# Norm factors with one token per partition, and spread back by a matmul with the identity

## The reference

```python
def rms_norm(x, g):
    xf = x.astype(jnp.float32)
    y = xf * lax.rsqrt(jnp.mean(xf * xf, axis=-1, keepdims=True) + NORM_EPS)
    return (y * g.astype(jnp.float32)).astype(x.dtype)
```

## Time and profile before

| | |
|---|---|
| median of 3 runs | 3188.65 us (3179.95 to 3190.11) |
| the profiled execution | 3185.06 us, span of its instructions 3183.4 us |
| mean granted clock | 0.978 |
| TensorE busy | 3001.6 us, 94% of the span |
| VectorE busy | 2112.0 us, 66% |
| ScalarE busy | 1008.0 us, 32% |
| chain that ended last | PE 88%, DVE 6%, ACT 3% |

### The profile page before, as it was taken

How to read it: one execution, slowest core, us unless ns; L and a number is a source line. 1 busy time by engine, 2 the same in 40 slices (tenths; PEclk the granted TensorE clock), 3 DMA queues, 4 the chain that set the end, 5 groups by cost and what they waited for, 6 DMA issues and landing times.

```text
span 3183.4 us, 46595 instructions
## 1 busy us (share of the span) xinstructions
PE 3001.6 (94%) x18188; PEld 2552.6 (80%) x18188; DVE 2112.0 (66%) x3065; ACT 1008.0 (32%) x1091; POOL 95.1 (3%) x154
## 2 busy tenths in 40 slices
PE   6999988999999999998999999989899989998898
PEld 4888856888868887784899899858779979985898
DVE  7877778667686766546566766646556666664466
ACT  5222223222232222314434444311033334342333
POOL 0000020000000000000000000000000000000000
PEclk9999999999999999999999999989999989999999
DMA  8444322434433433320345344400034554442244
GB/s 337 158 164 165 132 86 99 152 119 162 154 119 119 157 140 123 127 85 1 115 185 185 132 174 173 147 0 1 1 100 170 197 139 158 185 158 33 94 170 171
DMA packets 68214, 421.03 MB, mean 132 GB/s; under 512 B 7576, under 2 KB 8728, under 8 KB 25856
## 3 DMA queue, kind: packets, MB, share of 16 engines
q1 hardware_dynamic: 48416, 344.41, 29.3%
q0 software_dynamic: 19712, 75.41, 7.3%
HBM read 418.71 MB, written 1.07 MB: 132 GB/s over the span
## 4 chain that ended last, share of the span: by engine, by line
PE 88%; DVE 6%; ACT 3%; issue 1%; DMA 1%; SPq 0%; ACTq 0%; DVEq 0%
PE ps_o L1582 11%; PE ps_o L1584 10%; PE ps_o L1583 10%; PE ps_g L1582 7%; PE ps_u L1582 7%; PE ps_u L1584 7%; PE ps_g L1584 7%; PE ps_u L1583 7%; PE ps_g L1583 7%; PE ps_o L1589 2%; PE ps_g L1597 2%; PE ps_o L1775 1%; PE ps_o L1997 1%; DVE wlo L919 1%; ACT whi L605 1%
## 5 line engine op out<-in xcount | busy, mean ns | idle before, releaser
L605 ACT ACTIVATE whi<-wraw 128x2048 fp32r<-128x2048 f32 x326 | 622.2, 1912 | 1035.4 <-PE ps_u L1584 419.3
L919 DVE TENSOR_TENSOR wlo<-wraw,whi 128x2048 fp32r<-128x2048 f32 x326 | 738.6, 2289 | 211.0 <-ACT whi L605 210.7
L1582 PE MATMUL ps_o<-ah,wlo 128*128 128x256 f32 (+1 forms) x1408 | 468.9, 333 | 17.0 <-issue 15.4
L1582 PE MATMUL ps_g<-hh,wlo 128*128 128x256 f32 (+1 forms) x1408 | 460.0, 327 | 21.2 <-DVE hl L963 13.8
L1582 PE MATMUL ps_u<-hh,wlo 128*128 128x256 f32 (+1 forms) x1408 | 458.9, 326 | 0.0
L1584 PE MATMUL ps_o<-ah,whi 128*128 128x256 f32 (+1 forms) x1408 | 458.4, 326 | 0.0
L1584 PE MATMUL ps_u<-hh,whi 128*128 128x256 f32 (+1 forms) x1408 | 457.7, 325 | 0.0
L1583 PE MATMUL ps_o<-al,whi 128*128 128x256 f32 (+1 forms) x1408 | 457.7, 325 | 0.0
L1584 PE MATMUL ps_g<-hh,whi 128*128 128x256 f32 (+1 forms) x1408 | 457.2, 325 | 0.0
L1583 PE MATMUL ps_u<-hl,whi 128*128 128x256 f32 (+1 forms) x1408 | 456.8, 324 | 0.0
L1583 PE MATMUL ps_g<-hl,whi 128*128 128x256 f32 (+1 forms) x1408 | 456.4, 324 | 0.0
(11 more groups left out here) (381 smaller groups left out, 3890.5 us busy)
## 6 DMA issues: line engine op xcount, KB each, us to landing
wraw<-in_W SPq DMA_DIRECT2D x327, 1024.0 KB, 4.8
scr<-in_ADA POOLq DMA_DIRECT2D x120, 512.0 KB, 3.7
scr<-bias_rows POOLq DMA_DIRECT2D x8, 384.0 KB, 7.9
x<-in_XT POOLq DMA_DIRECT2D x1, 2048.0 KB, 10.6
x<-in_MEMT POOLq DMA_DIRECT2D x2, 1024.0 KB, 7.6
cst<-in_CST POOLq DMA_DIRECT2D x1, 1799.5 KB, 7.2
cst<-in_CB POOLq DMA_DIRECT2D x1, 1024.0 KB, 7.0
out<-x SPq DMA_DIRECT2D x1, 1024.0 KB, 4.8
```

Of the source, the lines that this page charges most:

```text
L605: nc.scalar.activation(whi[:, n % SLOTS, :], wraw[:, n % SLOTS, :], ACT.Copy).then_inc(w_hi, 1)
L919: tt_(wlo[:, n % SLOTS, :], wraw[:, n % SLOTS, :], whi[:, n % SLOTS, :].bitcast(f32), sub).then_inc(w_lo, 1)
L1582: mm(out, a[1], b[0], start=first, stop=False)
```

## The change

The sums are turned round. For each slice and each 128 tokens, the squares are the stationary operand and a single column of ones moves: the sum of token t lands in partition t, column q of `ps_g`. Root and reciprocal then work on 128 x 4 (or 128 x 2) numbers in `rcol` (columns 36 to 39 of `cols`). A matmul with the column repeated 128 times as stationary operand and the identity as moving one spreads each factor back over the partitions, into a PSUM bank (`ps_o` bank 0, or `ps_g` bank 1), which DVE reads directly in place of `rstd`. TensorE waits for the reciprocal between one filler and 2 (or 3) more. In norm 10 ACT also copies the factor to `rstd` for its second use, and in norms 8 and 11 the spreading stands after the second tile of the memory's key projection. The other sites only choose the bank.

```diff
@@ scalar: norm @@
-                    nc.scalar.activation(rstd[:, 0:N], ps_g[:, 0, 0:N], ACT.Sqrt, bias=C("eps", 1), scale=1.0 / D).then_inc(nm_std, 1)
+                    nt = N // 128
+                    nc.scalar.activation(rcol[:, 0:nt], ps_g[:, 0, 0:nt], ACT.Sqrt, bias=C("eps", 1), scale=1.0 / D).then_inc(nm_std, 1)
@@ scalar: norm 10 @@
             memory_std(1)
+            act.wait_ge(nm_back, st["k"])
+            nc.scalar.activation(rstd[:, 0:NX], RSTD_PROJECT[:, 0:NX], ACT.Copy).then_inc(nm_kept, 1)
@@ vector: norm @@
-                    nc.vector.reciprocal(rstd[:, 0:N], rstd[:, 0:N]).then_inc(nm_rstd, 1)
+                    nc.vector.reciprocal(rcol[:, 0:nt], rcol[:, 0:nt]).then_inc(nm_rstd, 1)
...
-                dve.wait_ge(nm_rstd, k + 1)
+                if again:
+                    dve.wait_ge(nm_kept, 1)
+                else:
+                    dve.wait_ge(nm_back, k + 1)
+                factor = rstd if again else bank
...
-                    stt(dst, src(d)[:, HALVES[j]], A(d, j), rstd[:, HALVES[j]], mult, mult).then_inc(nm_t, 1)
+                    stt(dst, src(d)[:, HALVES[j]], A(d, j), factor[:, HALVES[j]], mult, mult).then_inc(nm_t, 1)
@@ tensor: sum_squares @@
-                    ins = mm(ps_g[:, 0, 0:N], ones, tsq[:, d * NTOK:d * NTOK + N], start=d == 0, stop=d == KT - 1)
+                    for q in range(N // 128):
+                        ins = mm(ps_g[:, 0, q:q + 1], tsq[:, d * NTOK + 128 * q:d * NTOK + 128 * (q + 1)], ones[:, 0:1], start=d == 0 and q == 0, stop=d == KT - 1, skip_group_check=True)
...
+            def spread_factor(N, bank):
+
+                pe.wait_ge(nm_rstd, st["k"] + 1)
+                for q in range(N // 128):
+                    ins = mm(bank[:, 128 * q:128 * (q + 1)], rcol[:, q:q + 1].broadcast_to([128, 128]), ident, start=True, stop=True)
+                ins.then_inc(nm_back, 1)
@@ tensor: norm @@
                 if idle:
-                    keep_clock(N // 64 - 1 if part is None else 3, BANK[3])
+                    keep_clock(1, BANK[3])
+                if bank is not None:
+                    spread_factor(N, bank)
+                if idle:
+                    keep_clock(2 if part is None else 3, BANK[3])
@@ tensor: memory_kv @@
-                project(n, NX, t0=NX, then=lambda j: norm(NX, idle=False) if j == 0 else None)
+                project(n, NX, t0=NX, then=lambda j: sum_squares(NX, KT) if j == 0 else norm(NX, idle=False, bank=RSTD_PROJECT))
```

More of the change, by code:

```diff
@@ L310, in build @@
         nm_sq, nm_sum, nm_std, nm_rstd = sem("nm_sq"), sem("nm_sum"), sem("nm_std"), sem("nm_rstd")
+        nm_back, nm_kept = sem("nm_back"), sem("nm_kept")
         nm_t, nm_hi, h_ready = sem("nm_t"), sem("nm_hi"), sem("h_ready")
@@ L334, in build @@
         block = ctx.enter_context(nc.Block())
+        rcol = cols[:, 36:40]
+        RSTD_FFN, RSTD_PROJECT = ps_o[:, 0, :], ps_g[:, 1, :]
         def cut(tensor, first, count, pattern=None, **kw):
@@ L935, in memory_norm, with norm @@
                         tt_(hl[:, d - 3, NX:NTOK], mem_t[d - 3], hh[:, d - 3, NX:NTOK].bitcast(f32), sub).then_inc(me_ready, 1)
-            def norm(src, N, A, B, mode, part=None, again=False, early=False):
+            def norm(src, N, A, B, mode, part=None, again=False, early=False, bank=RSTD_FFN):
                 k = st["k"] - again
@@ L1244, in _ @@
             ffn(2, NTOK, gate(1, 0))
-            norm(xs_, NTOK, A_mod(1, 1), B_mod(1, 1), "split", part=3)
+            norm(xs_, NTOK, A_mod(1, 1), B_mod(1, 1), "split", part=3, bank=RSTD_PROJECT)
             def take_qkv(c, q, tile):
@@ L1299, in memory_chunks @@
                     split_lo(n + SLOTS)
-            norm(xs_, NX, gain("mix_norm_2", 0), None, "split", early=True)
+            norm(xs_, NX, gain("mix_norm_2", 0), None, "split", early=True, bank=RSTD_PROJECT)
             memory_chunks(0)
@@ L1519, in _ @@
                 tt_(rowb[:, 512 * g:512 * (g + 1)], BANK[1 + g][0:4, :], bt[0:4, 1536 + 512 * g:2048 + 512 * g], add).then_inc(bi_sb, 1)
-            norm(xs_, NX, gain("kv_norm_2"), None, "split")
+            norm(xs_, NX, gain("kv_norm_2"), None, "split", bank=RSTD_PROJECT)
             def take_kv(c, q, tile):
@@ L1541, in _ @@
             ffn(6, NX, half)
-            norm(xs_, NX, gain("mix_norm_2", 1), None, "split", early=True)
+            norm(xs_, NX, gain("mix_norm_2", 1), None, "split", early=True, bank=RSTD_PROJECT)
             memory_chunks(1)
@@ L1600, in sum_squares, with norm @@
                 st["sums"] = max(st["sums"], end)
-            def norm(N, split=True, part=None, again=False, idle=True):
+            def spread_factor(N, bank):
[3 more added lines that the diff above has]
+                ins.then_inc(nm_back, 1)
+            def norm(N, split=True, part=None, again=False, idle=True, bank=RSTD_FFN):
                 if again:
@@ L1816, in _ @@
             ffn(2, NTOK)
-            norm(NTOK)
+            norm(NTOK, bank=RSTD_PROJECT)
             n = FIRST["qkv", 0]
@@ L2137, in _ @@
             pe.wait_ge(bi_sb, 3)
-            norm(NX, idle=False)
+            norm(NX, idle=False, bank=RSTD_PROJECT)
             memory_sums(1)
```

## The result

| | before | changed |
|---|---|---|
| median of 6 runs | 3189.38 us (3179.95 to 3191.04) | 3199.38 us (3193.37 to 3203.22) |
| ratio, 95% interval | | 1.0035 (1.0019 to 1.0051) |
| the profiled execution, its span | 3185.06, 3183.4 us | 3198.93, 3197.3 us |
| mean granted clock of that execution | 0.978 | 0.966 |

The changed kernel is 10 us slower, where 23 was forecast.

What follows compares the result with a forecast made beforehand. TensorE, busy 94% of the span, and the places where it stands bound the kernel. 13.8 us saved at full clock became 24.4 lost with half clock: 3188.7 + 24.4 = 3213, stated as 3212, range 3174 to 3226.

Steps and rivals of the forecast that it cites:

- full-clock sum: All norms, with TensorE's clock taken as full throughout: the parts of the change together save 13.8 us.
- One sign: Sign that the forecast is right, in the norms: reciprocal and root take under 0.25 us each.
- The claim on the clock: TensorE's thin sums: weight loads with hardly a moving column neither hold nor win back the clock; 76 us more at 0.50.
- Rival 1: Thin passes hold the clock in all norms, so only the 13.8 us saving acts: 3175 us; chance 0.25.
- Rival 2: Clock falls only in long rows of thin passes, norms 1 to 4 and 7: about 0, 3188 us; chance 0.15.
- The condition: Stages whose first sum follows a wait: the first thin slice lengthens the lull by 0.45 us, to 2.5.
- the price of lost clock: All norms: half clock turns 13.8 us saved at full clock into 24.4 us lost.
- Norm 2: falls surely: Norm 2, first sum to spread factor: 13.4 us of full-clock work at half clock, +12.4; net 8.5 lost.
- now it doesn't come back while thin slices alternate with products: Woven sums after a wait: a fallen clock stays down, where before it came back in 3.4 us.
- some 2.2 each: Norms 1, 3, 4: filler, spreading and part of the sums at half clock take 2.2 us off each gain, leaving 2.5 together.
- at half clock every pass costs double: TensorE's passes at clock 0.50: six take 2.93 us where eight take 1.74 at full clock.
- two in three that it falls: Chance taken that the clock falls at a lull of 2.5 us; in norm 8, 4.6 us lost.

Runs made afterwards that it cites:

- changed again: The changed kernel unaltered, run and profiled once more: 3194.29 us, ratio 1.0012 to the kernel before.
- e1_wide: The changed kernel with 128 columns of ones moving in each pass of the sums instead of one: 3170.77 us, ratio 0.9940.
- e4_wide64: The changed kernel with 64 columns of ones moving in each pass of the sums instead of one: 3176.66 us, ratio 0.9955.
- e7_wide16: The changed kernel with 16 columns of ones moving in each pass of the sums instead of one: 3187.47 us, ratio 0.9996.
- e5_before_thin: The kernel before with one-column sums in slices 0 to 6 only, slice 7 alone making the factor, nothing spread: 3207.73 us, ratio 1.0052.
- e3_tail_wide: The changed kernel with 128 columns moving only in the sums at a norm's end, woven sums one column: 3182.97 us, ratio 0.9979.
- e2_woven_wide: The changed kernel with 128 columns moving only in the sums woven into products, those at the end one column: 3182.02 us, ratio 0.9971.
- e9_thin_lull: The changed kernel with two fillers ahead of the first woven sum in norms 2, 6, 8, 10 and 11: 3184.78 us, ratio 0.9980.

## Why the prediction was right in direction and wrong in size

Each norm, from its first sum to the first product of the next stage, against the same stretch of the kernel before; us, + is lost. Starts are read from one execution each, so a norm that loses the clock in one execution and not in the next shows here by chance.

| norm | forecast | changed | changed again | 128 columns |
|---|---|---|---|---|
| 0 | -1.1 | +1.8 | +1.4 | -1.4 |
| 1, 3, 4 together | -2.5 | -5.9 | -6.2 | -8.4 |
| 2 | +8.5 | +1.1 | -2.0 | -2.1 |
| 5, 9 together | -1.9 | -1.8 | -1.8 | -1.8 |
| 6 and 7 | +5.4 | +7.3 | +7.3 | -1.2 |
| 8 | +4.6 | +5.2 | +5.2 | +0.5 |
| 10 | +5.5 | +8.4 | +8.5 | 0.0 |
| 11 | +2.9 | +2.1 | -1.0 | -1.1 |
| 12 | +2.0 | -0.9 | -0.9 | -2.4 |
| sum | +23.4 | +17.4 | +10.5 | -17.9 |
| span, whole program | | +13.9 | +14.6 | -15.4 |

(The forecast's 1.0 us for woven sums at full clock comes on top, 24.4 in all. The 128-column kernel has the changed kernel's passes without its loss of clock: its column is to be read against the full-clock sum.)

**The full-clock sum held.** It was 13.8 us saved. The 128-column kernel saves 17.9 over the norms, 1.5 us of it each in norms 11 and 12 by a better clock in the woven part than that one execution of before had, so 14.9 without them. Norms 1, 3, 4 save 9.1 from the last product to the next stage's first, of 9.1; norm 2 2.2 of 2.24; norms 5 and 9 1.9 of 1.9. Norms 8 and 11 lose the 0.5 each that was taken (DVE's scaling starts 1.1 us later), and norm 10 nothing where 1.0 was. A thin slice costs what was taken, 0.87 us in the row of norm 2 for 0.89. One sign missed by a little: the root takes 0.26 us, not under 0.25.

**The claim on the clock held:** "a stream of weight loads with hardly a moving column doesn't hold or win back the clock". `e1_wide`, `e4_wide64`, `e7_wide16` and `e5_before_thin` show it, each by itself, and the total of half clock came out at 75 us for 76 between the two profiled executions. That the total fits is partly luck. By the mean clocks of the runs (0.976 before, 0.967 in six and 0.969 in twelve of the changed kernel) it is some 45 to 58 us more, an estimate from 2 x 0.007 x 3190 and 2 x 0.009 x 3190. Rival 1 has fallen in the kernel as changed; its 3175 is what 64 to 128 columns give. Rival 2 has half fallen: in norms 6 and 8 the woven sums keep the clock down (`e3_tail_wide`), but thin rows at the end alone cost 11 us (`e2_woven_wide`).

The condition was right in part. `e9_thin_lull` shows that the stand is needed in norms 6, 8 and 10. But the picture of a first thin slice that lengthens the lull and so brings the clock down doesn't fit norm 6, where it was down before that slice. The reading that the claim came from was mixed in the same way: TensorE stood 1.98 us ahead of the narrow passes of L1722, with 2.29 between weight loads, so those rows at 0.50 came after a stand and thin work, not after thin work alone.

The Trainium skill, TensorE: Matmul & The Clock Gate, Part 1, lets the clock go by how busy the array has been. That agrees if "busy" means data moving through it; read as TensorE's busy rows it is contradicted, by 10.00 busy of 10.00 us at clock 0.50 in norm 8.

**The step that failed** is the price of lost clock, 38.2 us (24.4 and the 13.8 saved). By the medians it is 28.6 (3199.4 less 3170.8), or 23.5 with the later runs. That is two thirds of the error of 14.4 us; the rest is that full clock gave 18.6 where 13.8 was forecast (3189.4 less 3170.8), and the 128-column kernel's clock, a little better than that of before (0.978 over the runs against 0.976), can account for nearly all of this: an estimate of 13 us less at 0.50 (2 x 0.002 x 3180), at 0.36 each. The result, 3199.4, lies 0.6 us under the forecast's own 3200 to 3224 and inside the stated range. Norm by norm, the column "changed" less the column "128 columns", against the same part of the forecast:

| norm | lost clock, forecast | changed | changed again |
|---|---|---|---|
| 0 | 0 | 3.2 | 2.8 |
| 1, 3, 4 | 6.6 | 2.5 | 2.2 |
| 2 | 10.7 | 3.2 | 0.1 |
| 6 and 7 | 6.8 | 8.5 | 8.5 |
| 8 | 4.1 | 4.7 | 4.7 |
| 10 | 4.5 | 8.5 | 8.5 |
| 11 | 2.4 | 3.2 | 0.1 |
| 12 | 3.0 | 1.5 | 1.5 |
| sum | 38.1 | 35.3 | 28.4 |

So in the first profile the sum is nearly right and its terms are not: norm 2 is down by 7.5 us, norms 1, 3, 4 by 4.1, and norms 0, 6 with 7 and 10 make up for 8.9 of it. That is luck. The terms that failed:

- "Norm 2: falls surely". In the first profile the clock did fall, at 497.9, but was back at 508.1, ahead of the row of sums at the end. In the second it held until 508.8 and was at 0.50 for 3.4 us in that row. "now it doesn't come back while thin slices alternate with products" is false there, and in norm 12, where it was back after 3.4 us (2986.2 to 2989.6). It is true in norms 6, 8 and 10. The working of that term is also off by itself: its parts (4 products of 1.29, 8 slices, filler, spreading) add up to 14.0 us, not 13.4.
- Norms 1, 3, 4, "some 2.2 each": the row of sums ran at 1.00, and one stretch of 3.4 us behind it at 0.50 (norm 1: 450.1 to 453.5), where DVE's scaling sets the pace for a good part: 0.7 to 1.1 each.
- "at half clock every pass costs double" was taken as a loss of half of every stretch. Between the profiles of 128 columns and of one, 82 us more at 0.50 (133.1 and 215.0) cost 29.3 us of span, 0.36 us for each; a line through the 18 executions of the changed kernel, span against time at 0.50 by the mean clock, gives 0.39. Norm by norm it is 0.41 to 0.47 in norms 2, 6 with 7, 8, 10, 11 and 12, and only 0.2 to 0.3 in norms 0 and 1, 3, 4. In part of the stretches TensorE waits anyway (2.5 of 23.7 us in norm 10); whether that is all of the gap no run separates.

On the other side, "two in three that it falls" was in norms 6, 8 and 10 every time in both profiles, and norm 10 lost nearly twice its term. Norm 0 lost 1.8 where 1.1 was to be gained, with the clock at 0.50 from 26.8 to 40.5; which of its waits carries that isn't worked out. The rest of the program, with nothing changed there, took 3.5 us less than before in the first profile and 4.1 more in the second.

**What stays open:** why norm 2 and norm 11 lose the clock in one execution and not in the next. The Trainium skill, TensorE: Matmul & The Clock Gate, Part 1, says of a kernel's start that the number of matmuls at the low clock varies from run to run of one kernel. Here the two profiles differ in the middle of the kernel (norm 2: 10.2 us at 0.50 in one, 3.4 in the other). And the 19 us of `e5_before_thin` against the 24 to 29 in the changed kernel: fillers, spreading and memory sums run in the same half-clock stretches there, but their share was not measured by itself.

## What to carry to other kernels

Turning a reduction round so that one result lies in each partition makes what follows it nearly free (root and reciprocal 38.0 us in sum before, 5.6 after), and a matmul with the identity brings it back for under 1 us. But with the squares as stationary operand a pass costs its weight load, whether 1 or 128 columns move: so move 128 columns of ones and not one, at the same time and with more of the clock kept. Where TensorE must stand ahead of thin work, put a filler into that stand (9.5 us here). And price lost clock place by place at what waits for it: here it cost 0.2 to 0.5 us for each us that it lasted, not 0.5 everywhere.

## What the runs showed of the hardware

- TensorE with its rows full (10.00 busy of 10.00 us, norm 8) was granted 0.50 for 10 us while one-column sums stood between its products; with 128 columns in those sums it had 1.00 for 10 us.
- The effect is graded: 1, 16, 64 and 128 columns at the same passes gave mean clocks of 0.968, 0.972, 0.976 and 0.978.
- One kernel's executions on one chip differ by 22 us (3181.83 to 3203.61), and the time follows the granted clock (0.972 to 0.965), while the 128-column kernel's six stay within 7 us.
- A reciprocal of 2 or 4 columns in 128 partitions takes 167 ns where 256 take 1752 and 512 take 3353.
